# Output projection in two pieces: 352-column products as 256 + 96 or 264 + 88 columns

## The reference

```
def finish(x, m, w_o, g_post_mix, g_pre_ffn, g_post_ffn, w_gate, w_up, w_down):
    x = x + rmsnorm(m @ w_o, g_post_mix)
    h = rmsnorm(x, g_pre_ffn)
    f = (jax.nn.silu(h @ w_gate) * (h @ w_up)) @ w_down
    return x + rmsnorm(f, g_post_ffn)
```

## Time and profile before

| | |
|---|---|
| median of 2 runs | 3081.24 us (3079.9 to 3082.59) |
| span of the profiled execution | 3082.5 us |
| TensorE matmul, busy | 3010.5 us, 98% of the span, 19766 |
| TensorE weight loads, busy | 2637.1 us, 86%, 19766 |
| VectorE busy | 1414.9 us, 46% |
| ScalarE busy | 1054.6 us, 34% |
| GpSimd busy | 759.0 us, 25% |
| mean granted TensorE clock | 0.993 |

### The profile page before, as it was taken

One profiled execution on the slowest core, in us unless ns is written; L12 is line 12 of the kernel. 1 busy time (PEld: TensorE's weight loads), 2 busy tenths in 40 slices (PEclk: granted clock), 3 DMA queues, 4 the chain that ended last, 5 costly groups with the idle time before them and its releaser, 6 DMA issues. The chain is left out here.

```text
span 3082.5 us, 48879 instructions
## 1 busy us (share of the span) xinstructions
PE 3010.5 (98%) x19766; PEld 2637.1 (86%) x19766; DVE 1414.9 (46%) x3330; ACT 1054.6 (34%) x2094; POOL 759.0 (25%) x546
## 2 busy tenths in 40 slices
PE   8999999999999999999999999999999999999998
PEld 6777766679999999999977777665899999999997
DVE  5579675466512112122565887654584111111125
ACT  4376535564311111011333665355642111110112
POOL 3002031324312122243500201312352122121132
PEclk9999999999999999999999999999999999999999
DMA  5120335651211111121321112457311111111131
GB/s 187 32 64 28 111 112 179 235 192 52 67 45 46 48 48 42 48 66 56 117 78 47 47 35 91 160 186 244 135 59 60 48 49 48 42 48 49 43 117 57
DMA packets 254072, 263.55 MB, mean 85 GB/s; under 512 B 24993, under 2 KB 224570, under 8 KB 253850
## 3 DMA queue, kind: packets, MB, share of 16 engines
q1 hardware_dynamic: 233370, 189.11, 19.6%
q0 software_dynamic: 20480, 71.32, 6.7%
HBM read 229.73 MB, written 30.65 MB: 84 GB/s over the span
## 5 line engine op out<-in xcount | busy, mean ns | idle before, releaser
L2231 PE MATMUL ps<-act_lo,w_hi 128*128 128x352 f32 x2112 | 683.5, 324 | 5.5 <-DVE act_lo L2698 3.8
L2231 PE MATMUL ps<-act_hi,w_hi 128*128 128x352 f32 x2112 | 677.1, 321 | 0.0
L2231 PE MATMUL ps<-act_hi,w_lo 128*128 128x352 f32 x2112 | 676.8, 320 | 0.0
L2608 POOL TENSOR_TENSOR w_lo<-w_raw,w_hi 128x1024 fp32r<-128x1024 f32 x132 | 322.0, 2441 | 1024.3 <-ACT w_hi L2449 1024.2
L740 PE MATMUL ps<-w_in_slots,hT 128*128 128x256 f32 (+1 forms) x2048 | 447.6, 374 | 4.9 <-PEq L206 3.2
L740 PEld LDWEIGHTS ps<-w_in_slots,hT 128*128 128x128 f32 x2048 | 373.5, 192 | 60.8 <-issue 10.6
L2231 PEld LDWEIGHTS ps<-act_lo,w_hi 128*128 128x128 f32 x2112 | 396.2, 188 | 11.1 <-DVE act_lo L2698 5.9
L2231 PEld LDWEIGHTS ps<-act_hi,w_hi 128*128 128x128 f32 x2112 | 396.9, 188 | 0.2
L2711 DVE TENSOR_TENSOR a_raw<-ps,silu 128x352 f32<-128x352 f32 x120 | 62.9, 524 | 726.7 <-PE ps L2231 726.6
L2231 PEld LDWEIGHTS ps<-act_hi,w_lo 128*128 128x128 f32 x2112 | 396.0, 187 | 0.0
L2231 PE MATMUL ps<-a_lo,w_hi 128*128 128x352 f32 x1056 | 344.0, 326 | 0.0
(11 more groups left out here) (371 smaller groups left out, 4271.7 us busy)
## 6 DMA issues: line engine op xcount, KB each, us to landing
w_raw<-in_w_gate SPq DMA_DIRECT2D x44, 512.0 KB, 3.8
w_raw<-in_w_up SPq DMA_DIRECT2D x44, 512.0 KB, 3.8
w_raw<-in_w_down SPq DMA_DIRECT2D x44, 512.0 KB, 3.8
w_in_slots<-in_w_in SPq DMA_DIRECT2D x18, 1024.0 KB, 5.3
xpark<-xT SPq DMA_DIRECT2D x9, 1408.0 KB, 5.6
xT<-xpark SPq DMA_DIRECT2D x6, 1408.0 KB, 14.4
hT<-xpark SPq DMA_DIRECT2D x6, 1408.0 KB, 12.8
wo_raw<-in_w_o SPq DMA_DIRECT2D x16, 512.0 KB, 5.3
```

The costliest lines, as they stand in the source:

```text
L2231: ins = pe.matmul(bank(b), w, x, start=first and i == 0, stop=end and i == 2)
L2608: pool.tensor_tensor(w_lo[slot(j)][:, 0:K, :], w_raw[slot(j)][:, 0:K, :], w_hi[slot(j)][:, 0:K, :].bitcast(F32), ALU.subtract).then_inc(w_ ...
```

## The change

`mix` no longer uses `terms` when `th` is 1 or 2. Each of the three matmuls of a product is issued as two, one after the other: columns 0 to 255 and 256 to 351 for `th == 1`, columns 0 to 263 and 264 to 351 for `th == 2`. Both go to the same bank, at their own columns, with the same weight. The start flag is set only on the first piece of the first term of k = 0. The first third (`th == 0`) and all later products stay as they were. The loops, the waits and the semaphores around them stay as well; the increment that tells ACT of a finished bank now hangs on the last, narrow piece.

```
             def mix(d, k, th):
-                return terms(d, wo_hi[:, k, d * P:(d + 1) * P], wo_lo[:, k, d * P:(d + 1) * P], act_hi[:, k, of(th)], act_lo[:, k, of(th)], k == 0, k == KC - 1)
+                rows, columns = slice(0, P), slice(d * P, (d + 1) * P)
+                if th == 0:
+                    return terms(d, wo_hi[:, k, columns], wo_lo[:, k, columns], act_hi[:, k, of(th)], act_lo[:, k, of(th)], k == 0, k == KC - 1)
+                wide = {1: 256, 2: 264}[th]
+                for i, (w, x) in enumerate(((wo_hi, act_lo), (wo_hi, act_hi), (wo_lo, act_hi))):
+                    for a, b in ((0, wide), (wide, TH)):
+                        ins = pe.matmul(ps[rows, d, a:b], w[:, k, columns], x[:, k, th * TH + a:th * TH + b],
+                                        start=k == 0 and i == 0 and a == 0, stop=k == KC - 1 and i == 2, skip_group_check=True)
+                return ins
```

## The result

The changed kernel takes 3133.31 us, the median of 2 runs (3132.43 and 3134.2), against 3081.24: 52.1 us more, a ratio of 1.0173 with a 95% interval of 1.0144 to 1.0203. In a later comparison, on a chip where the kernel before took 3107.79 us, it took 3158.98 in the median of 5, ratio 1.0168 (1.0154 to 1.0182). One of the 21 executions of the kernel before in that comparison took 7668.64 us, in a slow state, and is left out of the ratios. Forecast were 3135 us.

What follows compares the result with a forecast made beforehand. TensorE, busy 98% of the span, was taken as the bound: 768 splits at +72.7 ns give +55.8 us, less 2.0 us of vanished waits, so 3081.2 + 53.8 = 3135 us, range 3125 to 3180.

Steps and rivals of the forecast that it cites:

- What bounds the stage: Second and third thirds of the output projection: TensorE busy 64.01 of 65 us in layer 0, so added matmul time adds.
- The narrow piece is bound by a load, at 111 ns: Pieces of 96 or 88 columns, 40 or 37 ns, cannot cover the next weight load, so they step at 111 ns.
- The wide piece at 119.5 and 122.8 ns: Pieces of 256 and 264 columns step by their columns, 106.7 and 110 ns, plus 12.8 ns on top.
- The sum, 72.7 ns a split: Mean added time of wide plus narrow step over the former 159.5 ns; over 768 splits +55.8 us.
- The waits that go, 2.0 us: TensorE's waits for `w_lo` (0.7 us a layer) and before `mix_sum_2(1)` (0.3) vanish, giving back 2.0 us.
- The wait for `w_lo`: TensorE's wait at the end of the second third's norm chain, 0.7 us a layer, was to go.
- the wait for the root: TensorE's wait for ACT's root behind (1, 6), 0.9 us a layer, was to stay.
- Narrow pieces at the pace of four cycles a column: Rival: narrow fp32r pieces fall to plain fp32's pace, +96 us (3177) or +139 us (3220); chance 0.20.
- A hidden repeated load: Rival: the second piece's load of the same weight is hidden or not needed, 3081 to 3089 us; chance 0.07.
- The falling clock: Rival: TensorE's granted clock falls because columns pass more slowly, up to +217 us, near 3300; chance 0.04.
- What I said would show it: Profile signs at line 2245: steps of about 120 and 111 ns, 28 us more a layer, clock still at 1.00.
- narrow step of 40 to 55 ns: Sign in the changed kernel's profile that was to show the repeated load hidden or not needed.

Runs made afterwards that it cites:

- e5: Changed kernel with only the second third split (256 + 96), the third third as before: 3105.83 us against 3080.27, ratio 1.0087.
- e9: Changed kernel without its narrow pieces, leaving out columns from 256 or 264 to 351 of the two thirds: 3104.5 us against 3107.79, ratio 0.9993.
- e1: Changed kernel with both thirds cut 176 + 176 columns: 3128.36 us, ratio 1.0158 to the kernel before.
- e3: Changed kernel with only the first 32 of 128 weight columns in the wide piece, so its load is short: 3081.35 us, ratio 1.0005.
- e8: Kernel before with the plain fp32 matmuls of the input projection (line 743) split 256 + 96: 3101.31 us against 3080.27, ratio 1.0065.
- e4: Changed kernel with only the first 32 of 128 weight columns in the narrow piece: 3130.79 us, ratio 1.0168.
- e6: Changed kernel with both thirds in three pieces, 118 + 118 + 116 columns: 3213.82 us in the fastest execution, the others 3278.2, 3278.5 and 3345.8.
- e2: Changed kernel with both thirds cut 320 + 32 columns: 3153.11 us, ratio 1.024 to the kernel before.
- e10: Kernel before with the three terms of every split product in the opposite order: 3108.96 us, ratio 1.0007.

## Why the prediction was right, step by step

**What bounds the stage.** TensorE without a gap, so time added per matmul adds to the whole: right. Its two thirds are busy for 91.4 of 92.2 us as before, and e5 costs half of the change. The reverse, that time taken from a matmul shortens the stage, was not claimed, and e9 shows that it does not hold.

**The narrow piece is bound by a load, at 111 ns,** from eight plain fp32 matmuls of 32 columns. Right: by e1, e3 and e8, and in the changed kernel by the 0.11 us between the loads of a merged row. The narrow piece "cannot cover the next load", and the next load is that of a wide piece: it is this one that costs (e3). What the prediction left unsaid is that the added load, the narrow piece's own, is the covered one (e4). The sum does not change with it. The nearest row of another data type was a good price: 112 ns in e1.

**The wide piece at 119.5 and 122.8 ns,** its columns and the 12.8 ns that 352 columns have on top. Right: 119 ns in e9, 0.12 us in the changed kernel. This was the term with the widest bounds, 111 to 122. The plain fp32 row, with 3 ns on top, would have been the wrong one to take.

**The sum, 72.7 ns a split.** Measured were 70.5, the growth of the two thirds over their 384 splits, waits included, so 27.06 us a layer where 27.9 less the 0.3 of one vanished wait were expected. The 0.5 us between them are not traced further. That the whole came out within 2 us of 3135 says less than the steps do: the interval of the ratio, 1.0144 to 1.0203, allows 44 to 63 us more than before, and of the 4.0 us by which the two thirds grew more than the span 1.7 lie in the clock ahead of them, which the sum did not hold.

**The waits that go, 2.0 us.** They went, as forecast. In the changed kernel the sum inside (2, 6) follows its neighbours without a gap:

```profile
784.90 0.40 PE L2245 MATMUL ps<-act_hi,wo_lo 128*128 128x264 f32 x2
785.14 0.82 PE L2235 MATMUL ps<-y_odd,ones 128*128 128x352 f32 x2
```

This is a step of 0.24, where it was 0.45. The wait for `w_lo` is no longer among TensorE's waits, and the wait for the root has stayed, 1.6 us in two where it was 1.7:

```profile
PE ps L2245 <- ACT mix_rstd L2442: 1.6, 2, 0.8
```

The chain that ended last in layer 1 has become TensorE's own. The stretch of DVE, ACT and POOL from 2257 to 2298 us has nothing that answers to it; the rows that take its place are these:

```profile
2300.11 30.17 PE ps L2245 x258
2330.28 0.66 PE ps L2235 x2
2330.94 9.07 PE ps L2245 x78
2340.02 7.72 PE ps L2231 x48
2347.73 0.61 PE ps L2235 x2
2348.36 0.56 ACT mix_rstd L2442
```

**The rivals.** Narrow pieces at the pace of four cycles a column: fell with e1, at 112 ns a piece. What was said against it was in part misread: at 32 columns plain fp32 steps by the 111 ns of its load, so that row does not show two cycles a column; only those of 256 and 352 columns do. A hidden repeated load: the time fell with the result, +52 us and not +2 to +10. Half of its idea was true. The repeated load is hidden, and e4, where it has a quarter of the columns, is only 1 to 2 us faster; what costs is the next one. By the formula N / 2.4 + 2.5 of the Trainium skill's page "TensorE: Matmul & The Clock Gate", section "Back-to-back issue gap", a split would add 2.5 ns; 70.5 were measured. The section itself calls this the isolated gap, which leaves out the weight loads, and says that in a stream of loads and matmuls both set the spacing, so the prediction set it up as a stronger opponent than it is. The load time of the section "LDWEIGHTS (loading the stationary operand)", columns / 1.2, is 107 ns for 128 columns; the loads here step by 109 to 112 (e1, the changed kernel). The falling clock: not in the two thirds of this kernel, in none of seven executions by their times and mean clocks. Behind them, from 2375 to 2379 us, the profiled execution has a mean clock of 0.57, in a stretch with short waits for `act_lo`. And the reason I gave against the rival was weak. The attention had stayed at 1.00 with many narrow matmuls, and e6 shows a stretch with hardly any idle time that does not. The chance of 0.04 was for something that does happen one cut further on; that it happens for the reason given, the slower passing of columns, is not shown.

**What I said would show it.** The load steps of 111 and 120 ns are there. One sign was badly chosen: a "narrow step of 40 to 55 ns" was to speak for the hidden load. Read from the starts of the matmul records it would have been met: in the row of 709.85 above the two matmuls last 0.39 together and the narrow one 0.208, so it starts 0.18 us behind the wide one, and the next wide one, 0.23 behind the first, only 0.05 behind it. The load rows and the sum over a pair are the safe reading.

## What to carry to other kernels

In a dense stream a matmul that loads its weights costs the larger of its columns, with what comes on top of them, and the next load. For 128x128 weights of 4-byte type the load is about 110 ns at full clock here, the time of the columns alone of 264 columns of fp32r or 132 of plain fp32. Cutting a matmul costs next to nothing only as long as every piece covers the load behind it, as in e3, where that load was made short. Even cuts cost two loads (e1), uneven ones a load and the wide piece's columns (e2); the cheapest cut of these 352 columns that was tried, into halves, still cost 49 us for 768 of them. A stage in which TensorE is busy for 98% need not get shorter when TensorE gets faster: look at the chain of the other engines beside it first (e9).

## What the runs showed of the hardware that I had not expected

- The granted clock fell from 2.4 to 1.2 GHz in the middle of a stage in which TensorE is busy but for one wait of 0.8 us (e6), and stayed there for 140 us, at a price of 65 us; the same stage of the other layer held 2.4 GHz. The mean clocks of the four executions (0.994, 0.974, 0.973, 0.953) say that it fell in three of them. In the changed kernel (seven executions) and in e1 (four, 3126.25 to 3131.08 us) none stood apart. The cause is open.
- What an fp32r matmul takes on top of its columns, 12.8 ns in the mean for 352, is there for 256 columns as well (119 - 107 = 12 ns in e9). It stays with a short load beside it (e4) and with another order of the terms (e10), and it is gone at the lower clock, where 352 columns step by 293 ns. What it comes from is open; plain fp32, at two cycles a column, shows 3 ns.
- A matmul's record can begin while the record of its weight load still runs (by 0.14 us at 709.85 in the changed kernel), so starts of matmul records may alternate, 0.18 and 0.05 us, in a way that the columns, 107 and 40 ns, do not.
